# The tap sums of the Hyena filters, moved from inside a weight block of slot 6 to slot 8, into a bank of the lift

## The reference

```
h_full = concatenate([h[:, 0], zeros, reversed(h[1:, 1])])
h_full = h_full / jnp.sum(jnp.abs(h_full), axis=0, keepdims=True)
...
for n, gate in enumerate((x1, x2)):
    z_f = jnp.fft.rfft(z, n=2 * L, axis=1)
    conv = jnp.fft.irfft(z_f * filt_f[:, n], n=2 * L, axis=1)[:, :L]
    z = gate * (conv + bias[n] * z)
...
lifted = jnp.einsum('blnc,ncd->blnd', branches, w_lift[i])
gates = jax.nn.sigmoid(gate_logits.reshape(bsz, L, N_BRANCH, D_MODEL))
mixed = jnp.sum(gates * lifted, axis=2) @ w_out[i]
```

## Time and profile before

| | |
|---|---|
| Median of 3 runs | 2663.35 us (2663.02, 2663.35, 2667.92) |
| The profiled execution | 2667.16 us, span 2665.6 us, mean granted clock 0.988 |
| PE busy | 2585.6 us, 97% of the span |
| PEld, DVE, ACT busy | 2155.4, 1861.3, 1290.5 us |
| Share of PE in the chain that ended last | 90% |
| Tap sums (line 1891) | 64 matmuls in the profile, 16 at each of four places |
| Reciprocal (line 1109) | 4, 201 ns each |

### The profile page before, as it was taken

How to read it: one execution, slowest core, us unless ns; L and a number is a source line. 1 busy time by engine, 2 the same in 40 slices (tenths; PEclk the granted TensorE clock), 3 DMA queues, 4 the chain that set the end, 5 groups by cost and what they waited for, 6 DMA issues and landing times.

```text
span 2665.6 us, 41935 instructions
## 1 busy us (share of the span) xinstructions
PE 2585.6 (97%) x13736; PEld 2155.4 (81%) x13736; DVE 1861.3 (70%) x3251; ACT 1290.5 (48%) x2334; POOL 111.7 (4%) x206
## 2 busy tenths in 40 slices
PE   6999999999999999999989999999999999999998
PEld 5889999877776768898778999998867767688986
DVE  7788778735776867556678877887357768765666
ACT  5555555543444334443465555555334433444535
POOL 2100000000000000000021000000000000000000
PEclk9999999999999999999989999999999999999999
DMA  7544444434444335555464444444344534355554
GB/s 250 164 145 153 151 150 148 150 116 149 148 166 135 127 103 166 188 174 174 166 199 152 153 149 152 146 153 141 129 143 145 171 119 135 108 183 188 174 173 143
DMA packets 115956, 411.83 MB, mean 154 GB/s; under 512 B 15460, under 2 KB 15514, under 8 KB 115584
## 3 DMA queue, kind: packets, MB, share of 16 engines
q1 hardware_dynamic: 107424, 391.17, 44.1%
q0 software_dynamic: 8416, 19.18, 2.2%
HBM read 403.99 MB, written 6.29 MB: 154 GB/s over the span
## 4 chain that ended last, share of the span: by engine, by line
PE 90%; DVE 4%; issue 3%; ACT 2%; DMA 1%; PEldq 0%; PEld 0%; DVEq 0%; POOL 0%; ACTq 0%; POOLq 0%
PE bank L1620 28%; PE bank L1662 19%; PE bank L1664 10%; PE bank L2002 7%; PE bank L1577 5%; PE bank L1595 4%; PE bank L1752 2%; PE bank L1734 2%; PE bank L1715 2%; PE bank L1936 1%; PE bank L1922 1%; PE bank L1820 1%; PE bank L1700 1%; PE bank L1902 1%; DVE WL L395 1%
## 5 line engine op out<-in xcount | busy, mean ns | idle before, releaser
L381 ACT ACTIVATE WH<-ring 128x512 fp32r<-128x512 f32 x1364 | 856.0, 632 | 1156.2 <-PE bank L1620 494.2
L395 DVE TENSOR_TENSOR WL<-ring,WH 128x512 fp32r<-128x512 f32 x852 | 572.5, 689 | 439.5 <-ACT WH L381 436.7
L1662 PE MATMUL bank<-XX,WH 128*128 128x512 f32 x2304 | 821.4, 400 | 28.6 <-DVE XX L564 15.6
L1664 PE MATMUL bank<-XX,WL 128*128 128x256 f32 x2304 | 644.8, 280 | 0.0
L1662 PEld LDWEIGHTS bank<-XX,WH 128*128 128x128 f32 x2304 | 436.1, 189 | 129.4 <-DVE XX L564 15.6
L1620 PE MATMUL bank<-WH,XX 128*128 128x512 f32 x1536 | 492.2, 402 | 4.8 <-issue 3.4
L386 DVE TENSOR_TENSOR WL<-ring,WH 128x512 fp32r<-128x512 f32 x512 | 351.1, 688 | 138.7 <-ACT WH L381 134.8
L1664 PEld LDWEIGHTS bank<-XX,WL 128*128 128x128 f32 x2304 | 437.9, 190 | 0.0
L1620 PEld LDWEIGHTS bank<-WH,XX 128*128 128x128 f32 x1536 | 287.7, 190 | 85.9 <-issue 24.1
L1620 PE MATMUL bank<-WL,XX 128*128 128x512 f32 x768 | 302.7, 394 | 0.0
L1577 PE MATMUL bank<-ARENA,ring 128*128 128x256 f32 x704 | 159.0, 388 | 13.4 <-ACT ARENA L1365 11.1
(11 more groups left out here) (311 smaller groups left out, 3336.8 us busy)
## 6 DMA issues: line engine op xcount, KB each, us to landing
ring<-in_blocks SPq DMA_DIRECT2D x738, 512.0 KB, 3.3
ARENA<-in_bc POOLq DMA_DIRECT2D x2, 2048.0 KB, 8.9
ARENA<-in_decay POOLq DMA_DIRECT2D x8, 512.0 KB, 4.5
ARENA<-in_x SPq DMA_DIRECT2D x4, 512.0 KB, 9.4
u_scratch<-ARENA POOLq DMA_DIRECT2D x16, 128.0 KB, 2.5
ARENA<-u_scratch POOLq DMA_DIRECT2D x64, 32.0 KB, 3.3
y_scratch<-ARENA POOLq DMA_DIRECT2D x16, 128.0 KB, 2.0
ARENA<-y_scratch POOLq DMA_DIRECT2D x64, 32.0 KB, 2.7
```

The source lines that it names most:

```text
L381: nc.scalar.activation(wh[q], raw(which[0], q), ACT.Copy).then_inc(wh_ready[q], 1)
L395: vec.tensor_tensor(wl[q], raw(which[0], q), wh[q].bitcast(F32), ALU.subtract).then_inc(w_used[slot(which[0], half)], 1)
L1662: ins = mm(bank[b][:, :], h, xx[:, :, k, :], start=(k == 0), stop=(k == DT - 1), skip_group_check=True)
L1664: ins = mm(bank[b][:, 0:T], l, xh[:, k, :], start=False, stop=(k == DT - 1), skip_group_check=True)
```

## The change

`tap_sums` leaves block 6. PE now runs it in slot 8, after the forward transform and before block 8, into bank 2, which is empty then: group g of the lift has been read, and the next group's lifted branch begins in slot 10. DVE takes the reciprocal from bank 2 at the end of its slot 8 instead of slot 6. `between` disappears. Bank 4 has nine uses for each order now, bank 2 six in the stage, and `lifted` skips the two that belong to the sums. The number and the shapes of the instructions are the same.

```diff
-    "hyc":  [4, 4, 4, 4, 20, 18, 18, 18],
+    "hyc":  [4, 4, 6, 4, 18, 18, 18, 18],
...
-            at = {"taps": 2 * n, "dft": 2 * n + 1, "sums": 5, "turn": 4, "fwd": 5 + n, "inv": 7 + n}[step]
-            return o * 10 + at + (step in ("fwd", "inv")) if b == 4 else o * 9 + at
+            return o * 9 + {"taps": 2 * n, "dft": 2 * n + 1, "turn": 4, "fwd": 5 + n, "inv": 7 + n}[step]
+
+        def lifted(stage, b, g):
+
+            return g + (g + 1) // 2 if stage == "hyc" and b == 2 else g
...
-                        full(2 + t, "hyc", g)
+                        full(2 + t, "hyc", lifted("hyc", 2 + t, g))
...
-                        out_of(2 + t, "hyc", g)
+                        out_of(2 + t, "hyc", lifted("hyc", 2 + t, g))
...
-                    if s_ == 6:
-                        full(4, "hyc", hyc(o, "sums", 0, 4))
-                        free(v.reciprocal(NS[:, o * 8:o * 8 + 8], bank[4][:, 0:8]), 4)
+                    if s_ == 8:
+                        full(2, "hyc", 3 * o + 1)
+                        free(v.reciprocal(NS[:, o * 8:o * 8 + 8], bank[2][:, 0:8]), 2)
...
-                        if q == 2 and between is not None:
-                            between()
...
-                            take_bank(b + t, stage, g)
+                            take_bank(b + t, stage, lifted(stage, b + t, g))
...
-                    take_bank(4, "hyc", hyc(o, "sums", 0, 4))
+                    take_bank(2, "hyc", 3 * o + 1)
                     for j in range(8):
-                        ins = mm(bank[4][:, j:j + 1], SUM[:, j * P:(j + 1) * P], ones[:, 0:1], start=True, stop=True)
+                        ins = mm(bank[2][:, j:j + 1], SUM[:, j * P:(j + 1) * P], ones[:, 0:1], start=True, stop=True)
...
-                    done(ins, 4)
+                    done(ins, 2)
...
                     if s_ == 6:
                         turn_z(o)
-                        between = lambda: tap_sums(o)
...
                     if s_ in (8, 9):
                         forward(o, 1, s_ - 8)
+                    if s_ == 8:
+                        tap_sums(o)
```

More of the change, by code:

```diff
@@ L1623, in token_step, with token_block @@
                     return ins
-                def token_block(b, x, j, n, between, *which):
+                def token_block(b, x, j, n, *which):
                     for q in range(4):
-                        if q == 2 and between is not None:
-                            between()
                         part_made(q, *which)
@@ L1639, in token_block, with gated_block @@
                             ins[1].then_inc(parts_used[q], 1)
-                def gated_block(stage, g, p, x, y, *which, between=None):
+                def gated_block(stage, g, p, x, y, *which):
                     b = 0 if p < 4 else 2
@@ L1645, in gated_block @@
                         for t in range(2):
-                            take_bank(b + t, stage, g)
-                    token_block(b, y if b else x, p - 4 if b else p, 2 if b else 4, between, *which)
+                            take_bank(b + t, stage, lifted(stage, b + t, g))
+                    token_block(b, y if b else x, p - 4 if b else p, 2 if b else 4, *which)
                 def wide_half(b, half, *which):
@@ L1944, in _ @@
                     o, s_ = k // 12, k % 12
-                    between = None
                     if s_ in (0, 3):
@@ L1961, in _ @@
                         pe.wait_ge(yl_ready, layer * 4 + 2)
-                    gated_block("hyc", k // 6, k % 6, (xh, xl), yc, B_LIFT + 24 + k, between=between)
+                    gated_block("hyc", k // 6, k % 6, (xh, xl), yc, B_LIFT + 24 + k)
                 yb = (split(YBH, WT), split(YBL, WT))
```

## The result

The changed kernel takes 2646.36 us (median of 4 runs, 2646.26 to 2646.54), the kernel before 2665.64 us in 4 runs (2663.02 to 2671.27). The ratio is 0.9922, 95% interval 0.9909 to 0.9934. The profiled execution took 2646.54 us, with a span of 2645.0 us against 2665.6 and a mean granted clock of 0.991 against 0.988. Lines of the new kernel: 1892 is the sums, 1923 the forward transforms, 1911 the turn, 1937 the inverse transforms, 1623 the weight block, 1463 ACT's copy of z, 1112 the reciprocal.

What follows compares the result with a forecast made beforehand. PE was taken as the bound (97% busy, 90% of the chain). Terms of 11.1 + 6.9 + 0.9 + 1.0 = 19.9 us gave 2647.3 us; allowing for quicker runs, the forecast was 2646.5 us, range 2642 to 2651.

Steps and rivals of the forecast that it cites:

- The pauses: PE's waits ahead of the sums (4 x 1.2 us) and of slot 7's transforms (4 x 1.6 us) go: 11.1 us.
- The slow matmuls: In slot 6, the half block behind the sums (6.9 us) and the sums (0.9 us) stop running at the lower clock.
- The clock behind the sums in slot 8: Ahead of block 8: no clock fall expected, cost 0, with 0 to 2.56 us a place as bounds.
- the first rival: Clock falls behind the sums in slot 8: 6.7 us at all four places, 2653.2 us; at two, 2649.9; chance 0.13.
- DVE and the filled wait: Sums in slot 8 fill PE's wait for DVE ahead of block 9's third quarter: 4 x 0.24 = 1.0 us back.
- The sum: Whole kernel: 11.1 + 6.9 + 0.9 + 1.0 = 19.9 us off the profiled 2667.16 us, giving 2647.3 us.
- Slot 7's start: Slot 7's transforms: block 6 ends 0.17 us behind ACT's copies of z, so no new wait; bounds 0 and 1.2 us.
- the third rival: At slot 7, ACT's copy takes the reciprocal's place as the wait: 4.8 us, 2651.3 us; chance 0.05.
- The moved reciprocal: DVE's 0.2 us reciprocal between the WL of blocks 9 and 10 costs nothing; without cover 4 x 0.2 = 0.8 us.
- The transposes: Rival: slot 6's clock falls stay because of its 16 transposes; 6.9 us stay, 2653.4 us; chance 0.06.
- given back: Rival: PE, 5 us ahead at each place, meets something later that doesn't move; some 3 us left, 2660 us; chance 0.03.
- The slower rival: Sums in slot 8 lower the clock until slot 10: 14.8 us lost a place, 59 us in all, 2706 us; chance 0.03.

## Why the prediction was right

**The pauses, 11.1 us.** The mechanism was right: both rows are gone. The size was too small. PE's matmuls overlap: one takes 0.39 us and the next starts 0.23 us behind its start. The idle time of the rows begins at the end of the last matmul, so it leaves out the overlap that is lost as well. Place 4 of the kernel before, which has no fall, shows it in the starts:

```profile
2284.80 0.39 PE L1620 MATMUL bank<-WL,XX 128*128 128x512 f32 x1
2286.40 1.95 PE L1891 MATMUL bank<-CON,ARENA 128*128 128x1 f32 x16 [1.21 <-ACT ARENA L1460]
...
2290.81 0.39 PE L1620 MATMUL bank<-WL,XX 128*128 128x512 f32 x1
2292.76 3.70 PE L1922 MATMUL bank<-ARENA,CON 128*128 128x512 f32 x8 [1.56 <-DVE NS L1109]
```

From start to start that is 1.60 and 1.95 us where 0.23 is the pace: the pauses cost 1.37 + 1.72 = 3.09 us a place, 12.4 in all. The kernel with the sums in block 6 and bank 2 bears it out: at place 4 it is 3.33 us quicker than before, of which these 3.09 are the main part.

**The slow matmuls, 6.9 + 0.9 us.** Right for the profiled execution: block 6 takes 5.46 to 5.49 us at all four places. That the pause and the sums together caused the falls was an inference from four places; now it is shown. With neither pause and the sums where they were there was no fall at four places (bank 2), with the first pause and the sums there were four (earlier reciprocal), and a pause of 1.56 us without sums brought none. Runs of the kernel before differ, from 2660.21 to 2674.63 us over all its measurements; that those with fewer falls in slot 6 gain less follows from the account, but only one of them was profiled.

**The clock behind the sums in slot 8, taken at 0.** Right, in 20 places of five profiles with the sums once and whole. So the first rival did not come true. With sums twice as long it does at three places of four, at 1.6 us each, close to the 1.68 us that the earlier trace rows gave. The prediction's reason for 0, that the sums were shorter than every stretch behind which a row showed a fall, was drawn from few rows, hence the chance of 0.13.

**DVE and the filled wait, 1.0 us.** The mechanism was right, the size too small: 0.43 us a place, 1.7 us in all, outside the bounds of 0 and 1.0. I had read the wait off the starts of PE's matmuls as 0.24 us; the list of waits has 0.5 us for the load of the same matmul's operand. The sums in slot 8 also take 1.84 us, not 1.95, another 0.4 us in all.

**The sum.** 12.4 for the pauses, 7.8 for the slow matmuls, 1.7 filled and 0.4 for the sums, less 0.4 for ACT's copy (below), make 21.9 us; the changed stretch gives 21.6 where I had 19.9. That the median came out within 0.2 us of the forecast is partly luck: three terms were too small, the changed kernel's profile is 1.0 us late ahead of the first place, and I had set the forecast between two readings of the quicker runs, 0.8 us under what the profile gave.

**Slot 7's start.** The margin was called 0.17 us, and the copy is late by 0.1 us instead: 0.4 us in all, the small end of the third rival. The step at fault is the same overlap: I let the second half of block 6 begin at the end of the first half's last matmul, 0.16 us later than it does when nothing stands between. With the sums in block 6 and bank 2 the transform starts at the plain pace.

**The moved reciprocal, nothing.** Right. It stands at 883.66, and DVE then waits for ACT all the same:

```profile
883.66 0.20 DVE L1112 RECIPROCAL NS<-bank 128x8 f32<-128x8 f32 x1
883.78 0.64 DVE L398 TENSOR_TENSOR WL<-ring,WH 128x512 fp32r<-128x512 f32 x1
884.64 0.69 DVE L398 TENSOR_TENSOR WL<-ring,WH 128x512 fp32r<-128x512 f32 x1 [0.22 <-ACT WH L384]
```

**The other rivals.** The transposes stay in slot 6 after the change and keep no fall alive there. Nothing was given back later: the span is shorter by the 21.6 us of the four places less the 1.0 us ahead of the first. The slower rival needed a clock that stays down; behind the doubled sums it was down for 3.4 us and then back.

## What to carry to other kernels

A small piece of work that borrows the bank of a larger one inherits both of that bank's waits, the one for its last reader and the one that its own reader makes for the next writer. Look at what the matrix engine does around such a pause: here the clock fell where 1.95 us of matmuls of one column stood behind 1.2 us of idle time, and that cost 7.8 us beside the 12.4 us of the waits. Measure a pause from start to start, not by the idle time alone: two waits of 1.21 and 1.56 us cost 1.37 and 1.72. When the total varies by more than the effect, measure between two fixed instructions around the change.

## What the runs showed of the hardware

- The granted clock fell from 1.00 to 0.50 behind 3.6 us of float32 matmuls of one column each, in which the profile shows no idle time of PE, at 3 of 4 places (the sums twice), and at none of 20 places with 1.84 us of them.
- With 1.2 us of idle time ahead of 1.95 us of such matmuls it fell at 7 of 8 places (the kernel before and the one with the earlier reciprocal); each of the four in the latter lasted 3.4 us. Behind 1.56 us of idle time between full matmuls it stayed at 1.00 at 4 places (the kernel before).
- A stretch of 3.4 us at 0.50 cost 1.6 us of PE's row (the sums twice, place 2 against place 1).
- A pause of PE between float32 matmuls costs 0.16 us more than the idle time that the profile gives it, since a matmul of 512 columns takes 0.39 us and the next starts 0.23 us behind its start (1.21 us idle cost 1.37, 1.56 cost 1.72).
- 16 float32 transposes ahead of 1.84 us of sums, 3.5 us together, brought no fall in 4 places.
- A float32 matmul of one column against a 128 x 128 operand costs 1.81 / 8 = 0.23 us of PE's time (the sums twice), two instructions of 0.11 us.
